# Seven half-size products per panel pair in an up-projection, with the weight sums of the down-projection made elsewhere

## What is computed

```python
h = rms_norm(x, norm_ffn)                         # (1024, 1024)
u = h @ w_up                                      # w_up: (1024, 4096), gate | value
u = causal_conv3(u, conv_w) + conv_b              # per column, along the tokens
gate, val = jnp.split(u, 2, axis=-1)
x = x + (jax.nn.gelu(gate) * val) @ w_down        # w_down: (2048, 1024)
```

## Time and profile before

| what | value |
|---|---|
| median of 3 runs | 1425.19 us (1423.29 to 1426.36) |
| profiled execution | 1425.08 us, span 1423.3 us |
| TensorE busy | 1364.5 us, 7325 matmuls |
| VectorE, GpSimd, ScalarE busy | 744.9, 506.4, 401.8 us |
| granted clock of TensorE, mean | 0.988 of full |

### The profile page before, as it was taken

The page is one execution under the profiler, slowest core; times in us unless marked ns, Lnnn a source line. Parts: engine busy times, 40 slices in busy tenths (PEclk is TensorE's granted clock), DMA queues, the critical chain, the costliest instruction groups (busy, mean ns, idle before and its releaser), DMA issues.

```text
span 1423.3 us, 18467 instructions
## 1 busy us (share of the span) xinstructions
PE 1364.5 (96%) x7325; PEld 1088.9 (77%) x7325; DVE 744.9 (52%) x1215; ACT 401.8 (28%) x779; POOL 506.4 (36%) x270
## 2 busy tenths in 40 slices
PE   5999889999999989999899999999999999999998
PEld 4888556799787756666588888788888888888887
DVE  5797676533553776566545231533343333359842
ACT  5422553400221144444411010521111111144341
POOL 4212003134633111011133334346554554357652
PEclk9999999999999999999999999999999999999999
DMA  7420101042101100000002141432333333126324
GB/s 189 47 47 27 45 1 30 17 80 55 39 19 38 38 19 1 19 20 19 19 20 55 45 163 45 153 114 92 114 113 108 103 103 118 44 65 216 104 91 161
DMA packets 138794, 99.54 MB, mean 70 GB/s; under 512 B 40016, under 2 KB 114128, under 8 KB 138704
## 3 DMA queue, kind: packets, MB, share of 16 engines
q1 hardware_dynamic: 138720, 98.54, 23.4%
HBM read 81.61 MB, written 16.91 MB: 69 GB/s over the span
## 4 chain that ended last, share of the span: by engine, by line
PE 89%; DVE 6%; ACT 3%; issue 2%; DMA 0%; SPq 0%; ACTq 0%; DVEq 0%
PE ps L769 25%; PE ps L770 24%; PE ps L771 24%; PE ps L1249 3%; PE ps L1282 2%; PE ps L1266 2%; PE ps L1007 1%; PE ps L1024 1%; PE ps L1037 1%; PE ps L784 1%; DVE merged L1955 1%; DVE small L2147 1%; ACT arena L1391 1%; PE ps L981 1%; DVE arena L1707 1%
## 5 line engine op out<-in xcount | busy, mean ns | idle before, releaser
L769 PE MATMUL ps<-hTh,wh 128*128 128x512 f32 x1008 | 403.4, 400 | 2.7 <-ACT arena L1481 2.0
L669 POOL TENSOR_TENSOR wh<-raw,zero 128x1024 fp32r<-128x1024 f32 (+2 forms) x69 | 141.6, 2052 | 732.0 <-PE ps L771 716.4
L771 PE MATMUL ps<-hTh,wl 128*128 128x512 f32 x1008 | 394.9, 392 | 0.0
L770 PE MATMUL ps<-hTl,wh 128*128 128x512 f32 x1008 | 394.8, 392 | 0.0
L672 POOL TENSOR_TENSOR wl<-raw,wh 128x1024 fp32r<-128x1024 f32 (+2 forms) x77 | 208.3, 2705 | 99.2 <-ACT wh L1427 93.8
L769 PEld LDWEIGHTS ps<-hTh,wh 128*128 128x128 f32 x1008 | 190.5, 189 | 47.3 <-issue 7.3
L771 PEld LDWEIGHTS ps<-hTh,wl 128*128 128x128 f32 x1008 | 190.5, 189 | 40.8
L770 PEld LDWEIGHTS ps<-hTl,wh 128*128 128x128 f32 x1008 | 190.8, 189 | 37.3 <-issue 0.5
L771 PE MATMUL ps<-wh,hTl 128*128 128x512 f32 (+2 forms) x480 | 166.6, 347 | 0.0
L770 PE MATMUL ps<-wl,hTh 128*128 128x512 f32 (+2 forms) x480 | 166.5, 347 | 0.0
L769 PE MATMUL ps<-wh,hTh 128*128 128x512 f32 (+2 forms) x480 | 166.5, 347 | 0.0
(11 more groups left out here) (342 smaller groups left out, 1828.0 us busy)
## 6 DMA issues: line engine op xcount, KB each, us to landing
raw<-in_w_in SPq DMA_DIRECT2D x35, 512.0 KB, 3.9
raw<-in_w_up SPq DMA_DIRECT2D x32, 512.0 KB, 4.1
res<-in_w_down SPq DMA_DIRECT2D x16, 512.0 KB, 6.3
v_down<-res SPq DMA_DIRECT2D x16, 512.0 KB, 4.5
raw<-v_down SPq DMA_DIRECT2D x16, 512.0 KB, 3.6
raw<-in_w_down SPq DMA_DIRECT2D x12, 512.0 KB, 3.7
merged<-in_x SPq DMA_DIRECT2D x8, 512.0 KB, 7.8
raw<-in_w_out SPq DMA_DIRECT2D x8, 512.0 KB, 3.6
```

Source lines behind the costliest of these rows:

```text
L669: eng.tensor_tensor(wh[:, p, 0:n], raw[:, p, 0:n], zero1[:, 0:1].broadcast_to((P, n)), ALU.add).then_inc(s_hi[0], 1)
L769: mm(out_, ah, bh, start=first, stop=False, skip_group_check=True)
L770: mm(out_, ah, bl, start=False, stop=False, skip_group_check=True)
L771: return mm(out_, al, bh, start=False, stop=last, skip_group_check=True)
```

## The change

**Up-projection.** Each panel pair (two halves of the 1024 rows of `w_up`, gate and value columns) times the two halves of the tokens is now made by seven products of half size in place of eight. Left sides are quarters of h (`a11`, `a12`, `a22`) and three sums of them (`n2`, `s1`, `s4`), right sides blocks of `w_up` of 512 rows by 128 columns (`w11`, ... as 128x512 on the chip) and four sums, made in place by GpSimd for each pair (`weight_sum`). Each product is 12 matmuls into one PSUM bank. Results are combined in PSUM: ScalarE copies bank c21 to the chip (`copy_x`) three times and c12 to c22 (`copy_z`) once a pair, VectorE adds the copies (`up_add`) three times. The value half of `convw` is negated once, and `minus_gain2` is made once.

**Order.** A list `STREAM` interleaves the products of two pairs and the pieces of the down-projection. The weight parts go through a ring of five slots of 128x512: ScalarE makes the high part of piece n when piece n - 5 is used up, GpSimd the low part (before, GpSimd made both in the up-projection). Loads are of 256 KB, in five slots. Loops are written out.

**Entry.** GpSimd rebuilds h of the first token half as high + low (8 sums). The sums of quarters of h (`hx32`) are made by VectorE (12 instructions with both operands on the chip), their high parts `hxh` by ScalarE and their low parts `hxl` by GpSimd (8) and VectorE (4); GpSimd makes 4 low parts of h.

**act.** Only 10 x 1024 columns stay on the chip. Six of the first eight pairs' rows of act go to DRAM after they are made, and come back during the down-projection.

**Sums for the down-projection.** `load_v`, `sum_v` and `save_v` are moved to the merges and the output projection, in eight rounds of 128x512 blocks. `sum_v(e)` stands behind `split_panel(30 + e)` in GpSimd's list, `save_v(e)` and `load_v(e + 1)` behind the load of panel 32 + e in SyncE's.

**Down-projection.** The same seven products in another order (`DN_LEFT`, `DN_RIGHT`, `DN_OUT`), with the rows of act that come from DRAM used late.

```diff
-        act = sb("act", [P, 16, L], at=ffn)
+        act = sb("act", [P, 10, L], at=ffn)
...
+        hxh = sb("hxh", [P, 12, HALF], F32R, at=ffn)
+        plain = ExitStack()
+        hx32 = sb("hx32", [P, 12, HALF], at=plain)
+        plain.close()
+        hxl = sb("hxl", [P, 12, HALF], F32R, at=ffn)
...
+        act_back = sb("act_back", [P, 6, L], at=down)
+        res1 = sb("res1", [P, TB, HALF], at=down)
+        down.close()
+        x_copy = small
+        vsum = [arena2[:, HALF * i:HALF * (i + 1)] for i in range(4)]
...
+        STREAM = [(0, 0), (0, 1), (1, 0), (0, 2), (0, 3), (0, 4), (1, 1), (0, 5), (1, 2), (0, 6), (1, 3), (1, 4)]
+        for j in range(2, 16):
+            STREAM += [(j, 0), (j - 1, 5), (j, 1), (j - 1, 6), (j, 2), (j, 3), (j, 4)]
+        STREAM += [("dn", 0), (15, 5), ("dn", 1), (15, 6)] + [("dn", c) for c in range(2, NPIECE)]
+        AT = {piece: n for n, piece in enumerate(STREAM)}
...
+        W_STEPS = []
+        for n, (j, i) in enumerate(STREAM):
+            W_STEPS += [("sum", j, 2)] if i == 3 and j != "dn" else []
+            W_STEPS += [("low", n)]
+            if j != "dn":
+                W_STEPS += [("sum", j, 1)] if i == 1 else [("sum", j, 3), ("sum", j, 4)] if i == 4 else []
...
+            def load_v(e):
+                if e:
+                    eng.wait_ge(S("v_saved"), 64 * e)
+                for i, (k, g) in enumerate(((0, 0), (0, 1), (1, 1), (1, 0))):
+                    eng.dma_start(vsum[i], w_down[0, k * D + e * P:k * D + (e + 1) * P, g * HALF:(g + 1) * HALF]
+                                  ).then_inc(S("v_in"), 16)
+            def save_v(e):
+                eng.wait_ge(S("v_sum"), 4 * (e + 1))
+                for i, v in enumerate((0, 2, 1, 3)):
+                    eng.dma_start(v_dram[v, e * P:(e + 1) * P, :], vsum[i]).then_inc(S("v_saved"), 16)
...
+                if p == P_NSAMERGE + 2:
+                    eng.wait_ge(S("pT_ps"), NPC)
+                if P_NSAMERGE + 3 <= p < P_NSAMERGE + 11:
+                    save_v(p - P_NSAMERGE - 3)
+                if P_NSAMERGE + 2 <= p < P_NSAMERGE + 10:
+                    load_v(p - P_NSAMERGE - 2)
...
+            def sum_v(e):
+                w11, w12, w22, w21 = vsum
+                eng.wait_ge(S("v_in"), 64 * (e + 1))
+                for i, (to, a, b) in enumerate(((w11, w11, w12), (w12, w12, w22), (w22, w11, w22), (w21, w22, w21))):
+                    if i:
+                        eng.wait_ge(S("v_sum"), 4 * e + i)
+                    eng.tensor_tensor(to, a, b, ALU.add).then_inc(S("v_sum"), 1)
...
+                if P_NSAMERGE + 1 <= p < P_NSAMERGE + 9:
+                    sum_v(p - P_NSAMERGE - 1)
...
+            def weight_piece(n):
+                j, i = STREAM[n]
+                if j != "dn" and i == 3:
+                    weight_sum(j, 2)
+                weight_low(n)
+                if j != "dn" and i == 1:
+                    weight_sum(j, 1)
+                if j != "dn" and i == 4:
+                    weight_sum(j, 3)
+                    weight_sum(j, 4)
+            for n in range(3):
+                weight_piece(n)
...
+            eng.wait_ge(S("v_saved"), 512)
+            for c in range(KC):
+                eng.wait_ge(S("n2lo"), c + 1)
+                eng.tensor_tensor(hx32[:, c if c < 4 else c + 4, :], hTh[:, c, T0].bitcast(F32),
+                                  hTl[:, c, T0].bitcast(F32), ALU.add).then_inc(S("h_pool"), 1)
+            for n in (3, 4):
+                weight_piece(n)
+            for c in range(4):
+                eng.wait_ge(S("n2hi"), 22 + 2 * c)
+                for k in (c, 8 + c):
+                    eng.tensor_tensor(hxl[:, k, :], hx32[:, k, :], hxh[:, k, :].bitcast(F32), ALU.subtract
+                                      ).then_inc(S("h_pool"), 1)
+            weight_piece(5)
+            for c in range(4):
+                eng.wait_ge(S("n2hi"), 29 + c)
+                eng.tensor_tensor(hTl[:, c, T1], low32[:, c, T1], hTh[:, c, T1].bitcast(F32), ALU.subtract
+                                  ).then_inc(S("h_pool"), 1)
+            for n in range(6, len(STREAM)):
...
+            def up_product(j, i):
+                n = AT[j, i]
+                eng.wait_ge(S("fw_split"), W_COUNT["low", n])
+                bank = up_bank(j, ("c21", "c11", "c12", "c21", "c12", "c21", "c21")[i])
+                if j >= 2 and i < 3:
+                    eng.wait_ge(S("up_read"), 2 * (j - 2) + 1 + (i == 2))
+                if j == 1 and i in (1, 2):
+                    eng.wait_ge(S("n2lo"), 28 + i)
+                if i >= 3:
+                    eng.wait_ge(S("up_copied"), COPY_COUNT[j, {3: 1, 4: 2, 5: 3, 6: 5}[i]])
+                for kc in range(4):
+                    if j == 0:
+                        if i < 2:
+                            eng.wait_ge(S("n2lo"), max(2, 4 * i + kc + 1))
+                        elif i in (2, 6):
+                            eng.wait_ge(S("n2lo"), 19 + 3 * kc if i == 2 else 29 + kc)
+                        else:
+                            eng.wait_ge(S("h_pool"), {3: 9 + 2 * kc, 4: 10 + 2 * kc, 5: 17 + kc}[i])
+                    ah, al = h_block(UP_LEFT[i], kc)
+                    w = slice(w_slot(n).start + kc * P, w_slot(n).start + (kc + 1) * P)
+                    ins = mm3(ps[:, bank, :], whf[:, w], wlf[:, w], ah, al, kc == 0 and i < 3, kc == 3)
+                ins.then_inc(S("fw_used"), 1)
...
+            def copy_z(j):
+                used(eng, AT[j, 2])
+                if j < 2:
+                    eng.wait_ge(S("n2lo"), 32 - j)
+                eng.activation(ps[:, up_bank(j, "c22"), :], ps[:, up_bank(j, "c12"), :], ACT.Copy
+                               ).then_inc(S("up_copied"), 1)
...
+            for n in range(6, len(STREAM)):
+                weight_high(n)
+                for done in (0, 1) if n == 6 else (n - 5,):
+                    j, i = STREAM[done]
+                    if j != "dn" and i in (1, 3, 5):
+                        copy_x(j, i)
+                    if j != "dn" and i == 2:
+                        copy_z(j)
+                    if done and STREAM[done - 1] in [(a, 6) for a in range(16)]:
+                        gelu(STREAM[done - 1][0])
+                    if j != "dn" and i == 6:
+                        conv_first(j, 0)
+                        conv_first(j, 1)
+                    if j == 15 and 1 <= i < 4:
+                        dn_high(i - 1)
...
+            for c in range(4):
+                eng.wait_ge(S("n2hi"), 9 + c)
+                eng.wait_ge(S("h_pool"), c + 1)
+                stt(low32[:, c, T1], ps[:, n_bank(8 + c, "n2"), :], minus_gain2[:, c:c + 1], hx32[:, c, :],
+                    ALU.mult, ALU.add).then_inc(S("n2lo"), 1)
+            for c in range(4):
+                eng.wait_ge(S("n2hi"), 13 + c)
+                stt(hx32[:, 4 + c, :], ps[:, n_bank(12 + c, "n2"), :], gain2[:, 4 + c:5 + c], hx32[:, 4 + c, :],
+                    ALU.mult, ALU.subtract).then_inc(S("n2lo"), 1)
+            for c in range(4):
+                eng.wait_ge(S("n2lo"), 13 + c)
+                stt(hx32[:, c, :], hx32[:, c, :], -1.0, hx32[:, 4 + c, :], ALU.mult, ALU.subtract
+                    ).then_inc(S("n2lo"), 1)
+                eng.wait_ge(S("n2lo"), 17 + 3 * c)
+                eng.wait_ge(S("h_pool"), 5 + c)
+                stt(hx32[:, 8 + c, :], hx32[:, c, :], -1.0, hx32[:, 8 + c, :], ALU.mult, ALU.subtract
+                    ).then_inc(S("n2lo"), 1)
+                eng.wait_ge(S("n2hi"), 17 + c)
+                tt(hxl[:, 4 + c, :], hx32[:, 4 + c, :], hxh[:, 4 + c, :].bitcast(F32), ALU.subtract
+                   ).then_inc(S("n2lo"), 1)
...
+            def up_add(j, i):
+                if i == 4:
+                    used(eng, AT[j, i])
+                eng.wait_ge(S("up_copied"), COPY_COUNT[j, {1: 1, 4: 3, 5: 5}[i]])
+                to = ps[:, up_bank(j, {1: "c11", 4: "c12", 5: "c22"}[i]), :]
+                tt(to, to, x_copy[:, :], ALU.add).then_inc(S("up_add"), 1)
```

More of the change, by code:

```diff
@@ new lines, in program @@
+        for j in range(1, 16):
+            LOADS += [(j, "w21"), (j, "w12"), (j, "w22")] + ([(j + 1, "w11")] if j < 15 else [])
+        LOADS += [("dn", c) for c in range(NPIECE)]
+        FREED = []
+        for step in W_STEPS:
+            if step[0] == "low":
+                j, i = STREAM[step[1]]
+                FREED += [(step, (j, i))] if j == "dn" else [(step, (j, {5: "w12", 6: "w21"}[i]))] if i in (5, 6) else []
+            elif step[2] in (3, 4):
+                FREED.append((step, (step[1], {3: "w22", 4: "w11"}[step[2]])))
@@ new lines, in program, with raw_block @@
+        RAW_SLOT = dict(zip(LOADS[:5], (2, 3, 4, 0, 1)))
+        RAW_AFTER, RAW_COUNT, per = {}, {}, [16] * 5
+        for n, piece in enumerate(LOADS):
+            if n >= 5:
+                step, old = FREED[n - 5]
+                RAW_SLOT[piece], RAW_AFTER[piece] = RAW_SLOT[old], W_COUNT[step]
+            per[RAW_SLOT[piece]] += 16
```

(17 more changed lines are left out.)

476 lines of the change are left out of this document (233 added, 243 removed).

## The result

The changed kernel takes 1436.8 us (median of 4 runs, 1430.5 to 1438.9), the kernel before 1424.4 beside it. The ratio is 1.0078, 95% interval 1.0042 to 1.0115: slower, where 1418 and faster had been forecast. The profiled execution was the fastest of the four: 1430.5, span 1428.8. Its first 700 us, which the change does not touch, ran some 4 us ahead of the execution before (the last merges begin at 708.6 in place of 712.7); so stages are compared by their lengths.

What follows compares the result with a forecast made beforehand. TensorE's matmuls were taken to bound the kernel (busy for 96% of the span). Matmuls -43.5, entry +31.3, merges +3, handover +1 and clock +1 sum to -7.2: 1418 us from 1425.2, range 1403 to 1430.

Steps and rivals of the forecast that it cites:

- the merges: Merges: load, sum and store of w_down's sums circle at about 15 us a turn, delaying panel 38's split: +3 us.
- handover and clock: Up- to down-projection handover: pieces 6 and 7 wait for late act, +1; lower granted clock after the entry's gaps, +1.
- my forecast: Whole kernel: the main case, 1418 us, within 1411 to 1424; chance 0.50.
- the whole range: Whole kernel: 1403 to 1430 us, leaving out the best of the cheap-entry case and the bad half of the stalled-loop case.
- Matmuls: Up-projection: 1344 matmuls in place of 1536, 192 fewer at 0.2267 us each: -43.5 us.
- The loop without a wait: Loop over panel pairs: 19.04 us a pair and no wait, bounds 0 and 2 us in each of 14 pairs.
- Rival B: Panel-pair loop: weight_high on a late w21 holds copy_z; 1.5 us a pair gives 1439; chance 0.16.
- Two tiny instructions, nothing to 0.4: Handover and rest: the new minus_gain2 and negated convw cost nothing to 0.4 us.
- The entry: Start of the up-projection: 33.7 us of TensorE idle, less the old 2.4: +31.3 us.
- the 6 us of wait ahead of (1,1): Entry: TensorE waits 6 us ahead of product 1 of pair 1, until GpSimd's low half releases it.
- The turns between GpSimd and VectorE: Entry: instructions with SBUF operands take turns on the two engines, about 1.85 us for two 512-wide ones.
- Rival C: Merges: the circle of v takes 16.5 us a turn, 7 us more, 1425, no measurable change; chance 0.12.

Runs made afterwards that it cites:

- kernel 4: The changed kernel with its new 32-byte constant taking 64 bytes, so that every buffer behind it begins 32 bytes later: 1433.9 us, ratio 1.0063 to the kernel before.
- 7: The kernel before with 32 unused bytes a partition where the changed one has its new constant: 1425.9 us, ratio 0.9991.
- experiment 5: The changed kernel with ScalarE's copies ahead of its rounding of the next weights for the first two pairs: 1430.5 us, ratio 1.0031 to the kernel before.
- 2: The changed kernel without the sums of w_down's quarters (loads, sums and stores left out): 1426.6 us, ratio 1.0024 to the kernel before.
- 3: The changed kernel with two buffers for the sums of w_down's quarters in place of one: 1425.8 us, ratio 1.0008 to the kernel before.
- 6: The changed kernel with only the order of the tail altered (first down-projection pieces later, outputs added earlier): 1433.3 us, ratio 1.0033 to the kernel before.
- kernel 10: The changed kernel with all the mends together, and the second down-projection output added before piece pair 13 instead of 15: 1410.3 us, ratio 0.9893 to the kernel before.
- 1: The changed kernel run again unaltered, for a second trace and a tighter time: 1436.6 us, ratio 1.0080 to the kernel before.

## Why the prediction was wrong

The forecast was 1418 and 1436.8 was measured, 19 us more. Two terms of the sum were mis-sized and a third was left out: the merges (+3, measured +9.5 to +11.9), handover and clock together (+2, measured +10.1 in the tail), and the slower matmuls (0, measured +3.7). Either of the first two alone takes the time out of the 1411 to 1424 of "my forecast", and both together past the 1430 of the whole range. Each is told below with the step that failed.

- **Matmuls, -43.5: right.** 7133 records in place of 7325, and a pair at 19.04 us in kernel 4, in place of 21.76 (96 x .2267).
- **The loop without a wait: right.** Rival B didn't come: `copy_z` held no product in any of 14 pairs, and took 0.58 us, within the bounds given. **But the term left out a rate.** The sum took .2267 for every matmul from the earlier trace rows, where all operands are old buffers. "Two tiny instructions, nothing to 0.4" was the price of `minus_gain2`; its 32 bytes cost 3.7 us in the loop and 1.7 in the merges (which the changed kernel doesn't see, as the circle sets them). Experiments 4 and 7 show both.
- **The entry, +31.3: right in sum, and partly by luck.** (2,0) starts 73.1 and 73.6 us behind the first transpose where 73.4 was worked out. The turns between GpSimd and VectorE came as forecast (1.75 for 0.68, and 10.1 us of wait in (0,2)). But the last tile came at 14.2 behind the first transpose, in place of 18.8, and the 6 us of wait ahead of (1,1) weren't there. In their place (0,3) waited 7.3 us for a copy on ScalarE behind a weight that hadn't landed, and the low clock took some 3. That copy is the mechanism of rival B, in the entry instead of the loop; it is worth 3.5 us there (experiment 5). Errors of both signs cancelled.
- **The merges, +3: mis-sized, by 6.5 to 8.9.** The mechanism was forecast, a circle of load, sum and store that holds the split of panel 38; its length was not. The first step that failed is the price of the loads: 4.4 us for four was worked out from the 2.8 of quiet stores, and they took 5.4 to 6.5, while the stores took 4.1. (The terms given, 5.2 + 4.4 + 4.4, make 14.0, where the text has 14.4.) "About 15" a turn was 15.7, which is 3.7 us over five turns, and sum_v(2) itself began 3.0 us late, as its load, and not its split, came last. So TensorE waited 5.3 us for the split of panel 38, not 3. The stage is longer by 9.5 and 11.9 in the two traces. Of this 7.1 to 9.5 go with the circle (2 and 3): the wait, the granted clock of .50 behind it (3.9 us long in the first trace, which cost 1.9, and 5.8 in the second), and some of the panels before, one of which waits 0.9 in the second trace. Of the remaining 2.4, 1.7 are the placement and 0.7 the low clock at the start of the stage. Rival C, at 16.5 us a turn (0.12), is the same mechanism; what the turns cost lies between the two, and the clock behind the wait was in neither.
- **Handover and clock, +1 and +1: mis-sized, by 8.** The tail takes 166.9 to 170.7 us in the seven kernels that keep its order, for 157.8 of matmuls. TensorE is idle for 6.7 to 7.7 of it: 2.1 at the handover (2.3 in kernel 4), 3.4 to 4.4 at piece 16, 1.1 at piece 48 for the last output of the upper half. Another 2.4 to 5.2 are matmuls at the low clock behind these waits. The second step that failed: the forecast looked at the operands of pieces 6 and 7 alone. What was late was the low part for piece 0, which stood on VectorE behind the four taps and the product of pair 14 (the row below), and the additions of outputs, behind operands made up to three pairs ahead on a full VectorE. Experiments 6 and 10 take 5 of the 10 back by order alone. In kernel 10 the other 5 are 0.5 us at (15,6), 2.5 at piece 32 for an output, and 2.1 of low clock.

```profile
1257.63 4.51 DVE L2492 TENSOR_TENSOR hTl<-act,hTh 128x1024 fp32r<-128x1024 f32 x2
```

**The sum again:** -43.5 + 31.3 (entry) + 3.7 (rate) + 10.1 (tail) = +1.6 behind the first transpose, where the traces of the changed kernel and of 1, 2 and 3 give 511.3 in the mean against 510.0 before; with 9.5 to 11.9 for the merges, +11.1 to +13.5. Measured: +12.1 to +12.4.
